# Two-layer trunk of four gated mixers: rotated tensors split over 128 partitions and placed by DMA, differential values two steps later, gates waiting for one read

## What is computed

```python
for l in range(2):
    h = rms_norm(x, pre_norm_g[l])
    proj = h @ w_in[l]                      # columns of four mixers, their gates, four merge gates
    ya = rglru(xa, ga)                      # conv, block-diagonal gates r and i, scan
    yb = ssd(z, xbc, dt_raw)                # softplus(dt_raw + bias), decays, chunk products
    yc = swa(rope(qc), rope(kc), vc, gc)    # windowed attention, 16 heads of 64, 4 of keys
    yd = diff(rope(qd), rope(kd), vd, gd)   # softmax(q0 k0) - lam * softmax(q1 k1), 8 heads
    yproj = [y @ w_branch[l, n] for n, y in enumerate((ya, yb, yc, yd))]
    out = sum(sigmoid(merge_n + b_n) * yproj[n]) @ w_out[l]
    x = x + rms_norm(out, post_norm_g[l])
```

## Time and profile before

| | us |
|---|---|
| median of 3 runs | 1915.69 (1913.70 to 1916.15) |
| the profiled execution | 1916.71 |
| its span in the profile | 1914.8 |
| PE busy | 1890.6 |
| DVE, ACT, POOL busy | 1172.4, 992.4, 393.5 |

### The profile page before, as it was taken

The page is one execution under the profiler, slowest core; times in us unless marked ns, Lnnn a source line. Parts: engine busy times, 40 slices in busy tenths (PEclk is TensorE's granted clock), DMA queues, the critical chain, the costliest instruction groups (busy, mean ns, idle before and its releaser), DMA issues.

```text
span 1914.8 us, 27900 instructions
## 1 busy us (share of the span) xinstructions
PE 1890.6 (99%) x11048; PEld 1020.4 (53%) x11048; DVE 1172.4 (61%) x1555; ACT 992.4 (52%) x1912; POOL 393.5 (21%) x266
## 2 busy tenths in 40 slices
PE   7999999999999999999999999999999999999998
PEld 4446765455455664544454477554554555655443
DVE  6677556587436777654367765655873468776432
ACT  5674454465334666543356645544662356765421
POOL 0212021142222332111001130112332222321110
PEclk9999999999999999999999999999999999999999
DMA  6224334443334655434222252354333344554421
GB/s 191 88 88 150 104 106 138 121 122 90 109 105 131 155 128 165 112 132 146 59 67 88 72 166 89 106 150 120 110 105 110 113 137 126 148 138 116 165 84 44
DMA packets 264747, 224.68 MB, mean 117 GB/s; under 512 B 88400, under 2 KB 253226, under 8 KB 264618
## 3 DMA queue, kind: packets, MB, share of 16 engines
q1 hardware_dynamic: 264618, 222.90, 39.3%
HBM read 182.96 MB, written 2.16 MB: 97 GB/s over the span
## 4 chain that ended last, share of the span: by engine, by line
PE 87%; DVE 4%; ACT 3%; issue 2%; POOL 2%; DMA 1%; SPq 1%; DVEq 0%; ACTq 0%; POOLq 0%
PE PS L591 85%; POOL X L1694 1%; DVE Y L1338 1%; DMA X<-X 1%; PE PS L695 1%; DVE X L1338 1%; ACT Y L1077 1%; DVE wsp L1335 1%; SPq L512 1%; DMA stage<-w_in 1%; ACT Y L1078 0%; SPq L564 0%; POOL Y L1694 0%; PE PS L819 0%; ACT wsp L1000 0%
## 5 line engine op out<-in xcount | busy, mean ns | idle before, releaser
L591 PE MATMUL PS<-hT,wsp 128*128 128x512 f16 (+2 forms) x4968 | 1083.2, 377 | 1.0 <-ACT hT L981 1.0
L591 PEld LDWEIGHTS PS<-hT,wsp 128*128 128x128 f16 x4968 | 479.5, 98 | 562.8 <-issue 13.6
L1335 DVE SCALAR_TENSOR_TENSOR wsp<-stage,wsp 128x2048 f16<-128x2048 f32 x148 | 352.9, 2384 | 164.8 <-ACT wsp L1000 162.6
L591 PE MATMUL PS<-ys,wsp 128*128 128x512 f16 x1536 | 339.4, 379 | 0.0
L1000 ACT ACTIVATE wsp<-stage 128x2048 f16<-128x2048 f32 x148 | 281.3, 1901 | 46.6 <-PE PS L591 44.7
L591 PEld LDWEIGHTS PS<-ys,wsp 128*128 128x128 f16 x1536 | 149.4, 98 | 178.4 <-issue 4.1
L591 PE MATMUL PS<-wsp,hT 128*128 128x256 f16 x1728 | 193.2, 273 | 0.0
L591 PEld LDWEIGHTS PS<-wsp,hT 128*128 128x128 f16 x1728 | 168.6, 98 | 22.7 <-issue 2.3
L1003 ACT ACTIVATE X<-PS 128x512 f32<-128x512 f32 (+1 forms) x120 | 68.4, 593 | 140.5 <-PE PS L591 108.2
L1694 POOL TENSOR_TENSOR X<-X,K 128x1024 f32<-128x1024 f32 x26 | 62.7, 2412 | 351.3 <-DMA X<-X 351.3
L1694 POOL TENSOR_TENSOR M<-M,T 128x512 f32<-128x512 f32 x48 | 67.4, 1407 | 292.1 <-DVE T L1335 292.1
(11 more groups left out here) (195 smaller groups left out, 1974.4 us busy)
## 6 DMA issues: line engine op xcount, KB each, us to landing
stage<-w_in SPq DMA_DIRECT2D x120, 1024.0 KB, 5.0
stage<-w_branch SPq DMA_DIRECT2D x32, 1024.0 KB, 5.3
X<-X SPq DMA_DIRECT2D x120, 128.0 KB, 2.4
stage<-w_out SPq DMA_DIRECT2D x8, 1024.0 KB, 5.4
Y<-sums SPq DMA_DIRECT2D x8, 512.0 KB, 6.3
M<-sums SPq DMA_DIRECT2D x8, 512.0 KB, 5.9
Y<-Y SPq DMA_DIRECT2D x24, 128.0 KB, 3.2
xres<-x SPq DMA_DIRECT2D x4, 512.0 KB, 6.7
```

Of the source, the lines that this page charges most:

```text
L591: return pe.matmul(o, a, b, start=start, stop=stop, skip_group_check=True)
L1335: return dve.scalar_tensor_tensor(out=o, in0=a, scalar=c, in1=b, op0=op0, op1=op1)
```

## The change

Five edits:

1. **Rotation split.** `rotated_hi` on ACT writes one float16 tensor `rhi` over 128 partitions (in T[:, 512:1024]) with one copy. `rotated_lo` moves from POOL to DVE: one subtraction over 128 partitions into `rlo`, called between the two evacuations of a slot. SP places all quarters: four DMAs of 64 partitions for a q panel instead of two, eight for a k panel instead of four.
2. **Waits of the placement.** The waits for free attention buffers (`sw_s`, `df_s`, `ssd_out`) move from ACT to SP, ahead of these DMAs; ACT and DVE wait for the DMAs of the rotated panel before, since `rhi` and `rlo` are single.
3. **`VALUES_AT`** goes from 8 to 10.
4. **`gates`** of the first tile wait for `dt_taken`, which DVE's first read of bank 4 gives, in place of `dta_ready`.
5. **`load_norm(0)`**, which uses the half of T that `rhi` now takes, moves from SP's pass 14 to pass 18, with a wait for the placement of kc.

```diff
-VALUES_AT = 8
+VALUES_AT = 10
...
-        rlo = T[:, 0:512].bitcast(F16).rearrange("p (u s) -> p u s", u=2)
+        rhi, rlo = (T[:, a:a + 512].bitcast(F16).rearrange("p (u s) -> p u s", u=2) for a in (512, 0))
...
                     if p >= 4 and PANELS[p - 4][0] in ROTATED:
                         kind, i = PANELS[p - 4][0:2]
-                        sp.wait_ge(s["rope_hi"], at("rope_hi", 2 * rope_index(p - 4) + 2, layer))
-                        sp.wait_ge(s["rope_lo"], at("rope_lo", 2 * rope_index(p - 4) + 2, layer))
+                        sp.wait_ge(s["rope_hi"], at("rope_hi", rope_index(p - 4) + 1, layer))
+                        sp.wait_ge(s["rope_lo"], at("rope_lo", rope_index(p - 4) + 1, layer))
+                        if kind == "qc" and i == 0:
+                            sp.wait_ge(s["ssd_out"], at("ssd_out", 8, layer))
+                        if kind == "qc" and i >= 2:
+                            sp.wait_ge(s["sw_s"], at("sw_s", LOCAL_SCORES * (i - 1), layer))
+                        if kind in ("qd", "kd") and i >= 2:
+                            sp.wait_ge(s["df_s"], at("df_s", 8 * (i - 1), layer))
                         for t, (own, other) in enumerate(((slice(0, HD), slice(HD, P)), (slice(HD, P), slice(0, HD)))):
-                            if kind == "kc":
-                                moves = ((kC[other, t], kC[own, t]), (kloC[other, t], kloC[own, t]))
-                            elif kind == "kd":
-                                moves = ((kD[i % 2][other, t], kD[i % 2][own, t]), (kloD[i % 2][other, t], kloD[i % 2][own, t]))
+                            if kind in ("kc", "kd"):
+                                hi, lo = (kC, kloC) if kind == "kc" else (kD[i % 2], kloD[i % 2])
+                                moves = [(to[side, t], of[own]) for to, of in ((hi, rhi), (lo, rlo)) for side in (own, other)]
                             else:
-                                moves = (((qC if kind == "qc" else qD)[i % 2][other, t], by_chunks(kind, rlo[own])),)
+                                to = (qC if kind == "qc" else qD)[i % 2]
+                                moves = [(to[own, t], by_chunks(kind, rhi[own])), (to[other, t], by_chunks(kind, rlo[own]))]
                             for o, a in moves:
                                 sp.dma_start(o, a).then_inc(s["rope_stack"], 16)
...
                                 pe.wait_ge(s["wbd_in"], at("wbd_in", 64, layer))
-                                pe.wait_ge(s["dt_raw"], at("dt_raw", 1, layer))
-                                pe.wait_ge(s["dta_ready"], at("dta_ready", 1, layer))
+                                pe.wait_ge(s["dt_taken"], at("dt_taken", 1, layer))
...
                 def rotated_hi(p):
                     kind, i = PANELS[p - 1][0:2]
...
-                    for t in range(2):
-                        copy(dst[HD * t:HD * t + HD, t], by_chunks(kind, rcos[HD * t:HD * t + HD])).then_inc(s["rope_hi"], 1)
+                    n = rope_index(p - 1)
+                    act.wait_ge(s["rope_done"], at("rope_done", n + 1, layer))
+                    if n > 0:
+                        act.wait_ge(s["rope_stack"], at("rope_stack", stacked_after(n - 1), layer))
+                    copy(rhi, rcos).then_inc(s["rope_hi"], 1)
...
+                def rotated_lo(p):
+
+                    if p > 0 and PANELS[p - 1][0] in ROTATED:
+                        n = rope_index(p - 1)
+                        dve.wait_ge(s["rope_hi"], at("rope_hi", n + 1, layer))
+                        if n > 0:
+                            dve.wait_ge(s["rope_stack"], at("rope_stack", stacked_after(n - 1), layer))
+                        tt(rlo, rcos, rhi, ALU.subtract).then_inc(s["rope_lo"], 1)
...
                     middle(p)
+                    rotated_lo(p)
                     if p > 0:
                         evacuate(p, 1)
...
-                        rotated_lo(p - 1)
```

More of the change, by code:

```diff
@@ L107 @@
 LOCAL_OUT_AT = 8
+LOCAL_SCORES = 4
 HEADS_AT = 6
@@ L337, in program @@
                  "hi_done", "lo_done", "tile_done", "act_free", "dve_free", "gate_ready", "act_chain", "dve_chain",
-                 "pool_chain", "xn_T", "h_hi", "h_lo", "dt_raw", "sp_in", "sp_exp", "dta_ready", "cs_done",
+                 "pool_chain", "xn_T", "h_hi", "h_lo", "dt_raw", "dt_taken", "sp_in", "sp_exp", "dta_ready", "cs_done",
                  "cs_ready", "dec_ready", "lru_par", "conv_first", "lru_gates", "lru_a", "lru_v", "lru_w", "lru_a2",
@@ L535, in one_layer @@
                         sp.wait_ge(s["cs_rows"], at("cs_rows", 1, layer))
-                        load_norm(0)
                         sp.dma_start(sums[layer], csT).then_inc(s["rows_out"], 16)
@@ L1213, in rotated_hi @@
                     kind, i = PANELS[p - 1][0:2]
-                    dst = {"kc": kC, "qc": qC[i % 2], "qd": qD[i % 2], "kd": kD[i % 2]}[kind]
-                    if kind == "qc" and i >= 2:
-                        act.wait_ge(s["sw_s"], at("sw_s", 4 * (i - 1), layer))
-                    if kind in ("qd", "kd") and i >= 2:
-                        act.wait_ge(s["df_s"], at("df_s", 8 * (i - 1), layer))
-                    if kind == "qc" and i == 0:
-                        act.wait_ge(s["ssd_out"], at("ssd_out", 8, layer))
-                    act.wait_ge(s["rope_done"], at("rope_done", rope_index(p - 1) + 1, layer))
-                    for t in range(2):
-                        copy(dst[HD * t:HD * t + HD, t], by_chunks(kind, rcos[HD * t:HD * t + HD])).then_inc(s["rope_hi"], 1)
+                    n = rope_index(p - 1)
[3 more added lines that the diff above has]
+                    copy(rhi, rcos).then_inc(s["rope_hi"], 1)
                 def falls(q):
@@ L1396, in evacuate @@
                         if n >= 1:
-                            dve.wait_ge(s["rope_hi"], at("rope_hi", 2 * n, layer))
-                            dve.wait_ge(s["rope_lo"], at("rope_lo", 2 * n, layer))
+                            dve.wait_ge(s["rope_hi"], at("rope_hi", n, layer))
+                            dve.wait_ge(s["rope_lo"], at("rope_lo", n, layer))
                         link(tt(rcos, rraw, cosT.unsqueeze(1).to_broadcast([P, 2, S]), ALU.mult))
@@ L1526, in between @@
                         bias = rowp[:, R_DTB:R_DTB + 16].unsqueeze(1).to_broadcast([P, ST, 16])
-                        link(stt(spw[:, 0, 0:64].rearrange("p (c j) -> p c j", c=ST), PS[:, 4, 0:64].rearrange("p (c j) -> p c j", c=ST),
-                                 IWS, bias, ALU.mult, ALU.add))
+                        stt(spw[:, 0, 0:64].rearrange("p (c j) -> p c j", c=ST), PS[:, 4, 0:64].rearrange("p (c j) -> p c j", c=ST),
+                            IWS, bias, ALU.mult, ALU.add).then_inc(s["dt_taken"], 1)
+                        dve.wait_ge(s["dt_taken"], at("dt_taken", 1, layer))
                         link(dve.tensor_scalar(spw[:, 0, 64:72], colA[:, A_LAM:A_LAM + 8], -1.0, None, ALU.mult))
@@ L1701, in rope @@
                     tt(rswap, rswap, sinT.unsqueeze(1).to_broadcast([P, 2, S]), ALU.mult).then_inc(s["rope_sin"], 1)
-                def rotated_lo(p):
-                    kind, i = PANELS[p][0:2]
-                    n = rope_index(p)
-                    pool.wait_ge(s["rope_hi"], at("rope_hi", 2 * n + 2, layer))
-                    if kind in ("qc", "qd"):
-                        pool.wait_ge(s["rope_stack"], at("rope_stack", stacked_after(n - 1), layer))
-                    hi = {"kc": kC, "qc": qC[i % 2], "qd": qD[i % 2], "kd": kD[i % 2]}[kind]
-                    for t in range(2):
-                        own = slice(HD * t, HD * t + HD)
-                        dst = {"kc": kloC[own, t], "qc": rlo[own], "qd": rlo[own], "kd": kloD[i % 2][own, t]}[kind]
-                        tt(by_chunks(kind, dst), by_chunks(kind, rcos[own]), hi[own, t], ALU.subtract).then_inc(s["rope_lo"], 1)
-                        pool.wait_ge(s["rope_lo"], at("rope_lo", 2 * n + 1 + t, layer))
                 if layer > 0:
@@ L1790, in stacked_after @@
 def stacked_after(n):
-    return 64 + 32 * n + 32 * max(0, (n - 4) // 2)
+    return 128 + 64 * n + 64 * max(0, (n - 4) // 2)
 def by_columns(v):
```

9 lines of the change are left out of this document (6 added, 3 removed).

## The result

The changed kernel takes 1920.74 us (median of 8 runs, 1920.47 to 1922.41), the kernel before beside it 1915.91 us (8 runs, 1913.21 to 1916.84). The ratio is 1.003 with an interval of 1.002 to 1.004. By the bound of 0.2% it is slower, and it lies 6.2 us above the end of the predicted range. The profiled execution has a span of 1918.7 us against 1914.8.

The account below looks back on a forecast made before the run. PE is busy 99% of the span, so only its waits can go. 1916.7 - 2.5 (gates) - 9.1 (differential waits) + 0.6 (left over) + 5.7 (placement) = 1911.4 us profiled, 1910.3 as median; range 1905 to 1914.5.

Parts of the forecast that it names:

- gates: First gates of layer 1: with dt_taken PE starts at once and the whole 2.5 us wait goes.
- differential waits, less what is left: Differential stages of both layers: 9.1 us of PE's waits and lower clock go, 0.6 us remains.
- placement of k: Slots 53, 57, 61 of both layers: PE waits for eight moves behind the load, 5.7 us together.
- the differential stages thus hold 9.1 us to win: Both layers' differential stages: 2.18 + 3.59 us idle, 1.6 us for shortened matmuls, 1.7 us lower clock.
- DVE's subtraction: New low-half subtraction on DVE, `T<-X,T`: about 1.22 us, 26 times.
- What is left of the waits: Slots 50 and 56 of layer 1, 58 of layer 0: waits of 0.6 to 1.4 us remain, 0.6 taken.
- The slower rival: Rotation chain: eight moves hold SP's queue, quarters land late in ten odd slots 51 to 59; about 1921 us, chance 0.06.
- The condition I named: Sign that the forecast is wrong: POOL row `X<-X,K` starts more than 2 us later in its slot than before.

Follow-up runs that it names:

- four moves alone: Kernel before plus four further 64-partition moves at each kd panel, behind the load, their output unused: 1920.19 us against 1916.0, ratio 1.0021.
- step 10 alone: Kernel before with only VALUES_AT = 10, POOL's low halves and four placement moves kept: 1914.66 us, ratio 1.0.
- quarters between: Changed kernel with SP issuing the four quarters for rswap between a differential slot's two transposes instead of behind both: 1909.22 us, ratio 0.9971.
- both moves: Changed kernel with the quarters between the two transposes and the eight kd moves ahead of the weight load in SP's order: 1906.09 us, ratio 0.9951.
- four moves fewer: Changed kernel without the own halves of kd2 and kd3, four moves there instead of eight: 1917.37 us, ratio 1.0013.
- early quarters on the kernel before: Kernel before with only the four quarters for rswap issued between the two transposes: 1917.91 us against 1915.18, ratio 1.0017.

## Why the prediction was wrong

It gave 1910.3 us and 0.06 to slower; the result is 1920.7. Its terms, in the order of the sum:

| term | predicted | shown by |
|---|---|---|
| gates | -2.5 | -2.5, gates alone |
| differential waits, less what is left | -8.5 | -0.8 alone, +0.9 beside the split |
| placement of k | +5.7 | +4.2 for four moves alone; +6.9 for the whole split, DVE's delay included |

**The step that failed is "the differential stages thus hold 9.1 us to win".** It took each wait of PE for the exponentials as an event of its own, which 1.28 us of other work would fill. They were the place where a loop of several engines let PE feel its length. With step 10 alone PE's waits for the exponentials fell to 0.8 us and the clock held in the differential stages, but the time fell by 0.8 us only, and PE meets the chain at the placement and at DVE's read of the turned heads instead. That it is the chain is shown by the two edits of SP's order, which touch no arithmetic and take 14.7 us off the changed kernel, and by PE's share of the chain above, which goes from 15% and 14% to 100% and 68% with them. For the kernel before that share already stood at 27% in layer 0.

**The second failure is one sentence of the placement step:** that PE would come 10.0 us after the load "because transposes and load go out about 1 us earlier". They went out later. In the row above the load is issued at 639.16, 4.6 us after the slot's start; PE would have come at 649.74 - 2.3 = 647.4, 8.3 us after it. Measured from PE's first score of the slot, means over the places named, from the timelines:

| us from the slot's start | before | step 10 alone | changed | quarters between | both moves |
|---|---|---|---|---|---|
| rotated sum starts, odd slots 51 to 59 | 9.1 | 10.0 | 9.3 | 8.3 | 8.6 |
| load issued, slots 52, 56, 60 | 3.0 | 4.0 | 4.1 | 2.9 | 8.5 (moves first) |

Step 10 alone shows it without the new split: the chain keeps its pace, PE's slots get shorter, and so everything on the chain stands later against PE. The other half of the step was right. From load issue to the last landing it took 10.4 to 11.4 us at the six places (10.2 to 11.2 predicted). With 8.3 to 9.2 us of distance instead of 10.0, the six cost 10.6 us and not 5.7.

**Gates: right**, mechanism and size. PE runs through, with no idle time ahead of the first gates at 991.81, and DVE's read had been done at 988.4:

```profile
985.77 6.21 PE L600 MATMUL PS<-hT,wsp 128*128 128x512 f16 x28
991.81 1.02 PE L600 MATMUL PS<-M,Y 128*128 128x512 f32 x2
```

```profile
988.16 0.21 DVE L1338 SCALAR_TENSOR_TENSOR Y<-PS,rowp 128x64 f32<-128x64 f32 x1
```

**DVE's subtraction: right in size.** Groups by shape of the whole execution (as the earlier trace rows), 1.23 us each, 26 times; the 9.0 us are what DVE waits ahead of the 26 for ACT's copy:

```profile
L1341 DVE TENSOR_TENSOR T<-X,T 128x1024 f16<-128x1024 f32 x26 | 32.1, 1234 | 9.0 <-ACT T L1011 9.0
```

What it costs by itself was not separated from the moves and from the stretched pairs; 6.9 and 4.2 us are 2.7 apart, inside the intervals.

**What is left of the waits: too small, by a step that failed too.** I took 0.6 us, since POOL's leaving was to relieve DVE in three of the twelve odd slots and the new subtraction was to cost the others no more than 1.22 us. The stretched pair of low differences did go at these three (slot 49 of both layers, slot 51 of layer 0: 2.55 us before, 0.62 after). But it came at four others, slots 55 and 59 of both layers, because POOL's next job moved up beside it, as the run of the split alone shows. The three waits for the exponentials that are left, 0.3, 0.7 and 1.2 us, together 2.3, all stand in the slot behind such a pair (60 of layer 0, 56 and 60 of layer 1). The waits for DVE's read of the turned heads, another 0.9 us, were in no term.

**The slower rival** had the right chain and the wrong cause, so that its 1921 us meets the measured 1920.7 is luck. It wanted quarters held up by the moves' transfers by 2.5 us; the quarters were late because they stand behind the transposes, and PE had become earlier. The condition I named ("POOL row `X<-X,K` starts more than 2 us later in its slot") did occur, in slot 51 of layer 0: 630.53 is 8.2 us into the slot, 628.90 before was 6.2. There the issue came at the same time against PE as before (1.9 and 1.7 us), and the last quarter took 4.4 us to land against some 2.5 for the others. Why that one is slow in some slots and not in others stays open; in the run with four moves fewer the same slot had it at 6.2 us.

Also open: what the new split would cost with POOL's job of slots 55 and 59 kept behind DVE's pair, which no run tried, and why quarters and moves together bring the old split nothing beyond either (1910.3 and 1910.4 against 1910.7). In all three PE still waits 2.1 to 3.1 us for DVE's read of the turned heads.

## What to carry to other kernels

Ahead of filling a wait of the busiest engine, follow the chain behind it back for a whole period of the loop, to the DMA issue that starts it; if the chain is as long as the engine's period, the wait only moves. The view of the chain that ended last answers this before any edit: here it gave PE 27% of the stage of layer 0. More idle time of a second engine ahead of one line doesn't, as it may have moved there from another line. When work leaves an engine, look what stands behind it in that engine's list, and beside what it will now run. Then look at the order of the issuing queue: what stands in it behind a long load, or behind something that waits for another engine, may be the cheapest thing to move, but only together with the slack for what it overtakes.

## What the runs showed of the hardware

- A move of 64 partitions, 128 KB, lands 5.7 us after its issue behind a 1 MB load in the same queue (medians 5.6 to 6.1 at the six places), and 2.3 us after it ahead of the load; SP issues one each 0.63 us in both cases.
- Two DVE subtractions of 128x128 that take 0.62 us take up to 2.55 us where a subtraction on POOL runs beside them (64x1024 in the kernel before, 128x512 in the changed one).
- The same wait is followed by a lower clock in one execution and not in another. After the wait of some 2.4 us at the gates the granted clock of TensorE fell towards its 1.2 GHz level in the runs of step 10 alone (0.83 over 985 to 995, some 1.7 us lost), of the split alone (0.89) and of early quarters on the kernel before (0.84), and stayed at 1.00 in the profiled executions of the kernel before and of the added moves. A wait of 2.7 us at slot 53 of layer 1 in the changed kernel left it at 1.00. What decides isn't shown.
